# Down projection of two ConvGLU layers: 16 of 22 inner tiles by a seven-product scheme

## The chip, the cores and the metric

The kernel runs on one core of one Trainium2 chip. The metric is the device time of one execution in microseconds, the median of several runs. Engines are named TensorE (PE in the rows; PEld is its weight load), VectorE (DVE), ScalarE (ACT), GpSimd (POOL) and SyncE (SP), whose queue issues nearly all DMAs.

## The reference

One step of a two-layer encoder over 1024 prompt and 32 sample tokens, model width 1024, float32: a gated linear attention layer, then a latent attention layer, each followed by a ConvGLU of inner width 2816. The change touches the two ConvGLUs alone:

```python
def conv_glu(h, prev, w_in, conv_w, conv_b, w_out):
    g, u = jnp.split(h @ w_in, [D_FF], axis=-1)
    gc, new_prev = causal_dwconv(g, prev, conv_w, conv_b)
    return (jax.nn.gelu(gc, approximate=False) * u) @ w_out, new_prev
...
    x = x + o
    h = rmsnorm(x, norm_ffn[l])
    o, prev = conv_glu(h, ffn_prev0[l], w_ffn_in[l], ffn_conv_w[l], ffn_conv_b[l], w_ffn_out[l])
    x = x + o
```

## The kernel before, in words

Activations lie transposed in SBUF: rows of 128 features (KD = 8 for the model, NF = 22 for the inner width), T = 1056 token columns. Every product of two float32 operands is made of three float32r matmuls: each operand is split into a rounded part (hi, by a ScalarE copy) and a remainder (lo, by a subtraction on VectorE or GpSimd), and hi x hi, hi x lo and lo x hi are added in PSUM (`mm3`, L339, and `product`, L752).

A ConvGLU runs as a list of units. Unit f makes gate and up rows of inner tile f. Unit 0 is plain. Units 1 to 21 use a seven-product scheme (Winograd's form of Strassen's): the operand x is a 2 x 2 block matrix of 4 rows by 528 columns, the weights likewise with gate and up as the two output rows. Four sums of weight quarters (`s_sums`, L978, VectorE) and four sums of x blocks, T1 to T4 (once per layer), feed seven products P1 to P7 of 24 matmuls of 128x264, in the order of `ORDER`: P1, P2, P6, P5, P7, P4, P3. ScalarE copies three results out of PSUM (`snap`), VectorE adds the others (`gate_left`, `up_right`, `up_left`, `gate_right`), then come the convolution (`conv`, L1070, VectorE, five operations), the GELU (ScalarE) and the product with up (`glu`, VectorE). SP stores the finished activation of each tile in DRAM (`sp_a_out`, L659, to s_a). x itself has been stored in DRAM (s_x), since the scratch of the units covers its rows in SBUF.

The down projection (`pe_ffn`, L867) then goes over 11 groups of two inner tiles. For each group SP loads 1 MB of weights and the two activations (`sp_a_in`), ScalarE and GpSimd split both, and TensorE makes 24 output tiles of 128x352 (8 rows, three column chunks), 6 matmuls each, 144 a group. VectorE adds each tile to x; in the first group it adds to x read back from DRAM into two places of 4 rows (xback), which SP loads during unit 21.

Two weight slots alternate over units and groups. The order of each engine is written out by hand; engines wait for each other by counting semaphores. SP's queue too is in program order: a wait in it (`prod(f, n)`: product number n of unit f is done) holds all DMAs behind it.

## Time and profile before

| | |
|---|---|
| median of 3 runs | 2638.41 us (2638.26 to 2638.42) |
| the profiled execution | 2640.56 us, its span 2638.7 us |
| TensorE's mean granted clock in it | 0.995 of full speed |
| matmuls | 18206 |
| DMA | 221.93 MB, mean 84 GB/s |

The span is the time from the first to the last instruction. The profile gives each engine's busy time, the chain of waits that ended last, groups of instructions by source line, and the issue of DMAs with their time to landing. Durations of matmuls overlap each other, so what a matmul costs is read from how many fit in a stretch of time.

### The profile page before, as it was taken

How to read it: one execution, taken by the hardware profiler on the slowest of the kernel's cores; microseconds unless marked ns; L12 is line 12 of the kernel's file. 1: busy time of each engine (PE TensorE's matmuls, PEld its weight loads, DVE VectorE, ACT ScalarE, POOL GpSimd, SP SyncE). 2: the span in 40 equal slices, each digit the busy share in tenths (PEclk: the TensorE clock that was granted, in tenths of full speed). 3: DMA queues.
4: the chain of work that ended last, by engine and by line, in shares of the span. 5: the costliest groups of instructions: out<-in, count | busy, mean ns of one | idle time of the engine just before them, and what ended most of it. 6: DMA issues, size and time to landing. Idle time of an engine off the chain costs nothing.

```text
span 2638.7 us, 43372 instructions
## 1 busy us (share of the span) xinstructions
PE 2579.3 (98%) x18206; PEld 2500.3 (95%) x18206; DVE 1487.2 (56%) x2660; ACT 1000.7 (38%) x1651; POOL 932.6 (35%) x546
## 2 busy tenths in 40 slices
PE   8999999999999999999999989999999999999999
PEld 7999999999999999999998988889999999999999
DVE  6735353578555455555625875555696555446554
ACT  6333333364233322111547756444453233321111
POOL 5121212152433444444522223223334433444441
PEclk9999999999999999999999999999999999999999
DMA  3111111122222224222213253132122222233222
GB/s 110 35 37 35 37 39 34 38 98 81 81 74 90 74 81 180 74 98 98 70 45 126 108 198 124 49 98 73 61 71 82 81 73 89 74 136 117 98 98 100
DMA packets 182159, 221.93 MB, mean 84 GB/s; under 512 B 16690, under 2 KB 145344, under 8 KB 181328
## 3 DMA queue, kind: packets, MB, share of 16 engines
q1 hardware_dynamic: 179567, 217.08, 24.5%
q8 instruction: 144, 2.36, 0.4%
q10 hardware_dynamic: 2400, 2.10, 0.3%
q14 instruction: 48, 0.39, 0.0%
HBM read 160.56 MB, written 58.59 MB: 83 GB/s over the span
## 4 chain that ended last, share of the span: by engine, by line
PE 89%; DVE 6%; ACT 2%; issue 1%; DMA 1%; SPq 0%; POOL 0%; DVEq 0%; ACTq 0%; POOLq 0%
PE ps L341 14%; PE ps L343 13%; PE ps L342 13%; PE ps L758 11%; PE ps L760 11%; PE ps L759 11%; PE ps L2366 3%; PE ps L1289 1%; PE ps L2350 1%; PE ps L1276 1%; PE ps L1277 1%; PE ps L1278 1%; DVE xT L585 1%; PE ps L1365 1%; PE ps L1348 1%
## 5 line engine op out<-in xcount | busy, mean ns | idle before, releaser
L585 DVE TENSOR_TENSOR xT<-xT,ps 128x352 f32<-128x352 f32 x672 | 347.2, 519 | 249.2 <-PE ps L343 248.1
L1170 POOL TENSOR_TENSOR wlo<-wraw,whi 128x1024 fp32r<-128x1024 f32 x78 | 187.3, 2401 | 454.7 <-DVE s_raw L993 454.7
L306 POOL TENSOR_TENSOR wlo<-wraw,whi 128x2048 fp32r<-128x2048 f32 (+1 forms) x37 | 168.3, 4550 | 498.2 <-ACT whi L299 468.8
L341 PE MATMUL ps<-fahi,whi 128*128 128x352 f32 x960 | 311.1, 324 | 0.1
L343 PE MATMUL ps<-fahi,wlo 128*128 128x352 f32 x960 | 308.1, 321 | 0.0
L342 PE MATMUL ps<-falo,whi 128*128 128x352 f32 x960 | 307.9, 321 | 0.0
L299 ACT ACTIVATE whi<-wraw 128x2048 fp32r<-128x2048 f32 x40 | 76.6, 1914 | 396.7 <-DMA wraw<-w_ffn_out 328.1
L341 PE MATMUL ps<-hh,whi 128*128 128x352 f32 x648 | 218.5, 337 | 0.6 <-ACT cqr L2679 0.3
L343 PE MATMUL ps<-hh,wlo 128*128 128x352 f32 x648 | 208.2, 321 | 0.0
L342 PE MATMUL ps<-hl,whi 128*128 128x352 f32 x648 | 207.9, 321 | 0.0
L758 PE MATMUL ps<-hh,whi 128*128 128x264 f32 x672 | 191.5, 285 | 0.4 <-DVE wlo L1019 0.4
L759 PE MATMUL ps<-hl,whi 128*128 128x264 f32 x672 | 191.2, 285 | 0.0
L760 PE MATMUL ps<-hh,wlo 128*128 128x264 f32 x672 | 191.2, 284 | 0.0
L341 PEld LDWEIGHTS ps<-fahi,whi 128*128 128x128 f32 x960 | 180.1, 188 | 0.9 <-DVE xT L585 0.4
L342 PEld LDWEIGHTS ps<-falo,whi 128*128 128x128 f32 x960 | 180.4, 188 | 0.2
L343 PEld LDWEIGHTS ps<-fahi,wlo 128*128 128x128 f32 x960 | 180.3, 188 | 0.0
L1170 POOL TENSOR_TENSOR s_lo<-s_raw,s_hi 128x512 fp32r<-128x512 f32 x80 | 148.4, 1855 | 60.0 <-ACT s_hi L890 60.0
L1047 DVE TENSOR_TENSOR hf<-hf,ps 128x528 f32<-128x528 f32 x42 | 29.6, 704 | 188.6 <-ACT hf L926 188.6
L758 PEld LDWEIGHTS ps<-hh,whi 128*128 128x128 f32 x672 | 126.5, 188 | 1.3 <-DVE wlo L1019 0.8
L341 PEld LDWEIGHTS ps<-hh,whi 128*128 128x128 f32 x648 | 121.6, 188 | 5.7 <-issue 2.6
L760 PEld LDWEIGHTS ps<-hh,wlo 128*128 128x128 f32 x672 | 126.6, 188 | 0.0
L759 PEld LDWEIGHTS ps<-hl,whi 128*128 128x128 f32 x672 | 126.4, 188 | 0.0
(414 smaller groups left out, 7920.0 us busy)
## 6 DMA issues: line engine op xcount, KB each, us to landing
wraw<-w_ffn_in SPq DMA_DIRECT2D x88, 512.0 KB, 3.8
s_a<-hf SPq DMA_DIRECT2D x44, 528.0 KB, 3.3
wraw<-w_ffn_out SPq DMA_DIRECT2D x44, 512.0 KB, 4.3
fa<-s_a SPq DMA_DIRECT2D x40, 528.0 KB, 6.1
wraw<-w_gla_in SPq DMA_DIRECT2D x24, 512.0 KB, 4.6
s_x<-xT SPq DMA_DIRECT2D x6, 1408.0 KB, 5.8
xback<-s_x SPq DMA_DIRECT2D x4, 2112.0 KB, 12.1
s_k<-kw SPq DMA_DIRECT2D x8, 784.0 KB, 3.3
```

Source lines behind the costliest of these rows:

```text
L299: act.activation(hi[:, 0:cols], raw[:, 0:cols], ACT.Copy).then_inc(S("w_hi"), 1)
L306: pool.tensor_tensor(lo[:, 0:cols], raw[:, 0:cols], hi[:, 0:cols].bitcast(F32), ALU.subtract).then_inc(S("w_lo"), 1)
L341: nc.tensor.matmul(out, w[0], x[0], start=start, stop=False)
L342: nc.tensor.matmul(out, w[0], x[1], start=False, stop=False)
L343: return nc.tensor.matmul(out, w[1], x[0], start=False, stop=stop)
L585: dve.tensor_tensor(xT[:, m, tc(j)], xT[:, m, tc(j)], ps[:, banks[i % len(banks)], 0:TC], ALU.add)\
L758: nc.tensor.matmul(out, w_[0], x_[0], start=first, stop=False, skip_group_check=True)
L759: nc.tensor.matmul(out, w_[0], x_[1], start=False, stop=False, skip_group_check=True)
L760: last = nc.tensor.matmul(out, w_[1], x_[0], start=False, stop=(k == HK - 1), skip_group_check=True)
L1047: dve.tensor_tensor(right, left, two(U_SIDE), ALU.add).then_inc(S("summed"), 1)
L1170: return pool.tensor_tensor(lo[:, cols], raw[:, cols], hi[:, cols].bitcast(F32), ALU.subtract)
L2366: last = pe.matmul(ps[:, 6, 0:m], av[h % 2][0:n, kk0 // P, :], aPT[s % 2][0:n, i, 0:m], start=(i == 0), stop=(i == len(tiles) - 1))
```

## The change

Inner tiles 1 to 16 of the down projection now go through the same seven-product scheme, in two chunks of eight inner tiles (ND = 8 units a layer, units 22 to 29; four per chunk, each unit making one pair of output rows, `PAIRS`). The x operand of a chunk is again a 2 x 2 block matrix: X11 and X21 are odd and even inner tiles, left half of the columns, X22 the even tiles' right half, T1 to T4 their sums. The sums are made by VectorE in the gate/up phase (`pair_sum`, four operations of 528 columns for each two units) and stored in DRAM (s_t). At the turn from unit 21 to 22, and from 25 to 26, SP loads seven blocks of 4 rows by 528 columns (`sp_block`) into the places of the old operands, each after the product that last reads the place; ScalarE rounds them (`refill`), VectorE subtracts for five of them and GpSimd for T3 and X22 (`block_lo`). No result is copied out of PSUM: VectorE adds the products straight into x (`into_x`, seven adds of 528 columns a unit). x is read back into its own rows in four pairs (`sp_x_in`). The other six inner tiles (0 and 17 to 21) stay plain, as three groups of two. In the down units VectorE makes all weight sums and remainders; their places are parts of the activation rows (S4), of x operand rows (S2, S3) and of the convolution's row (S3 of odd units).

Each unit's weight sums wait as the diff shows: for units 22 and 23 (`f in (NF, NF + 1)`) the fourth sum waits until all stores of even, or odd, tiles have landed, since it writes into those activation rows.

```diff
+        PAIRS = ((3, 4), (0, 1), (2, 5), (6, 7))
+        BLOCKS = (("X11", "X21", "T2", "T1", "T3", "T4", "X22"), ("X11", "X21", "T2", "T1", "T3", "X22", "T4"))
...
+        def sp_block(sp, layer, part, i):
+
+            name, n = BLOCKS[part][i], 7 * part + i
+            if A_LOADS * layer + n >= 2:
+                before, count = load_count(layer, n - 2)
+                sp.wait_ge(S(before), nth(before, count))
+            if name[0] == "T":
+                sp.wait_ge(S("t_stored"), nth("t_stored", 16 * (NT * layer + 4 * part + 4)))
+                src = A["s_t"][4 * part:4 * part + 4, :, ("T1", "T3", "T2", "T4").index(name), :].rearrange("q p t -> p q t")
+            else:
+                odd = name == "X11"
+                sp.wait_ge(S(f"a_stored{int(odd)}"), nth(f"a_stored{int(odd)}", 16 * (NFG * layer + 4 * part + 4 + (not odd))))
+                first, t0 = ND * part + (1 if odd else 2), TH if name == "X22" else 0
+                src = A["s_a"][first:first + ND - 1:2, :, t0:t0 + TH].rearrange("q p t -> p q t")
+            sem, _ = load_count(layer, n)
+            sp.dma_start(xblock(name)[1], src).then_inc(S(sem), 16)
...
-            sp_a_in(sp, layer, 0)
+            sp_block(sp, layer, 0, 0)
+            prod(f, 2)
+            sp_block(sp, layer, 0, 1)
+            sp_next_w(sp, layer, c0, f + 2, 0)
+            sp_x_in(sp, layer, 0)
             prod(f, 3)
-            sp.dma_start(xback[0][:, :, :], A["s_x"][:, 0:HK, :]).then_inc(S("x_back0"), 16)
+            sp_block(sp, layer, 0, 2)
             sp_a_out(sp, layer, f - 1)
-            prod(f, 4)
-            sp_a_in(sp, layer, 1)
-            prod(f, 5)
-            sp.dma_start(xback[1][:, :, :], A["s_x"][:, HK:KD, :]).then_inc(S("x_back1"), 16)
-            prod(f, 6)
-            sp_w_out(sp, layer, c0, 1)
+            for n in (4, 5, 6):
+                prod(f, n)
+                sp_block(sp, layer, 0, n - 1)
+            sp_next_w(sp, layer, c0, f + 2, 1)
+            prod(f, 7)
+            sp_block(sp, layer, 0, 6)
+            sp_x_in(sp, layer, 1)
+            sp.wait_ge(S("conv"), NF * layer + NF - 1)
+            sp_x_in(sp, layer, 2)
+            for f in range(NF, NF + ND):
+                last = f == NF + ND - 1
+                for n in range(1, 8):
+                    if n in (2, 7) or f == NF + 3 or last and n in (3, 4):
+                        prod(f, n)
+                    if f == NF + 3:
+                        sp_block(sp, layer, 1, n - 1)
+                    if last and n in (3, 4):
+                        sp_a_in(sp, layer, n - 3)
+                    if n in (2, 7):
+                        sp_next_w(sp, layer, c0, f + 2, n // 7)
+                if f == NF:
+                    sp.wait_ge(S("conv"), NF * (layer + 1))
+                    sp_x_in(sp, layer, 3)
+                    sp_a_out(sp, layer, NF - 1)
             sp_a_in(sp, layer, 2)
-            sp_a_out(sp, layer, f)
-            for g in range(2, NFG):
-                sp.wait_ge(S("down_mm"), 24 * (b0 + g - 1))
-                sp_w_out(sp, layer, c0, g)
-                if g > 2:
-                    sp_a_in(sp, layer, g)
+            sp.wait_ge(S("down_mm"), 24 * (b0 + 1))
+            for kk in range(2):
+                sp_w_out(sp, layer, c0, 2, kk)
...
-            for g in range(1, NFG - 1):
-                pe_down_ffn(pe, layer, chunk(c0 + NF + g), 24 * (b0 + g), g)
-            pe_down_ffn(pe, layer, chunk(c0 + NF + NFG - 1), 24 * (b0 + NFG - 1), NFG - 1,
+            for f in range(NF, NF + ND):
+                pe_unit_down(pe, layer, chunk(c0 + f), f)
+            pe.wait_ge(S("summed"), cnt("summed", layer, NF + ND - 1, 6))
+            pe_down_ffn(pe, layer, chunk(c0 + NF + ND), 24 * b0, 0, banks=FIRST_BANKS)
+            pe_down_ffn(pe, layer, chunk(c0 + NF + ND + 1), 24 * (b0 + 1), 1)
+            pe_down_ffn(pe, layer, chunk(c0 + NF + ND + 2), 24 * (b0 + 2), 2,
...
+            def refill(part, f, early, late):
+
+                block_hi(part, 0)
+                early()
+                block_hi(part, 1)
+                side_hi(f, "S2")
+                late()
+                block_hi(part, 2)
+                block_hi(part, 3)
+                w_hi_side(f)
+                block_hi(part, 4)
+                side_hi(f, "S3")
+                side_hi(f, "S4")
+                block_hi(part, 5)
+                block_hi(part, 6)
...
+                if 2 < f < NF:
+                    dve.wait_ge(S("prod"), cnt("prod", layer, f - 1, 0))
+                if f == NF:
+                    dve.wait_ge(S("t_stored"), nth("t_stored", 16 * NT * (layer + 1)))
+                if f > NF:
+                    dve.wait_ge(S("prod"), cnt("prod", layer, f - 1, 3))
+                if f == NF + 1:
+                    dve.wait_ge(S("glu"), NF * (layer + 1))
                 dve.tensor_tensor(s3, w[0], w[2], ALU.subtract).then_inc(S("s_sum"), 1)
-                dve.wait_ge(S("s_sum"), nth("s_sum", 4 * u + 1))
+                dve.wait_ge(S("s_sum"), cnt("s_sum", layer, f, 1))
                 dve.tensor_tensor(w[2], w[2], w[3], ALU.add).then_inc(S("s_sum"), 1)
-                dve.wait_ge(S("s_sum"), nth("s_sum", 4 * u + 2))
+                dve.wait_ge(S("s_sum"), cnt("s_sum", layer, f, 2))
                 dve.tensor_tensor(s2, w[2], w[0], ALU.subtract).then_inc(S("s_sum"), 1)
-                dve.wait_ge(S("s_sum"), nth("s_sum", 4 * u + 3))
+                dve.wait_ge(S("s_sum"), cnt("s_sum", layer, f, 3))
+                if f in (NF, NF + 1):
+                    stored = f"a_stored{f % 2}"
+                    dve.wait_ge(S(stored), nth(stored, 16 * NFG * (layer + 1)))
                 dve.tensor_tensor(s4, w[1], s2, ALU.subtract).then_inc(S("s_sum"), 1)
...
+                s_sums(f + 1)
+                if f == NF - 1:
+                    w_low_in(f + 1)
+                    block_lo(0, 0)
+                    block_lo(0, 1)
+                pair = (f - 3) // 2 if f % 2 and f <= 2 * NT + 1 else None
+                if pair is not None:
+                    pair_sum(pair, "T1")
+                    pair_sum(pair, "T3")
+                up_right(f)
+                if f == NF - 1:
+                    block_lo(0, 2)
+                up_left(f)
+                if pair is not None:
+                    pair_sum(pair, "T2")
+                    pair_sum(pair, "T4")
+                gate_right(f)
+                if f < NF - 1:
+                    conv(f)
+
+            for f in range(NF, NF + ND):
+                part, first, more = (f - NF) // 4, (f - NF) % 4 == 0, f + 1 < NF + ND
+                side_lo(f, "S2")
+                if first:
+                    into_x(f, 1)
+                    block_lo(part, 3)
+                w_low_side(f)
+                if not first:
+                    into_x(f, 1)
+                side_lo(f, "S3")
+                if f == NF:
+                    conv(NF - 1)
+                into_x(f, 2)
+                if f > NF:
+                    side_lo(f, "S4")
+                into_x(f, 3)
+                if f == NF:
+                    side_lo(f, "S4")
+                if first:
+                    into_x(f, 4)
+                    block_lo(part, BLOCKS[part].index("T4"))
+                    if f == NF:
+                        glu(NF - 1)
+                    into_x(f, 5)
                     s_sums(f + 1)
-                up_right(f)
-                up_left(f)
-                gate_right(f)
-                conv(f)
-
+                    into_x(f, 6)
+                    w_low_in(f + 1)
+                    into_x(f, 7)
+                    continue
+                if more:
+                    s_sums(f + 1)
+                into_x(f, 4)
+                if f == NF + 3:
+                    block_lo(1, 0)
+                    into_x(f, 5)
+                    w_low_in(f + 1)
+                    block_lo(1, 1)
+                    into_x(f, 6)
+                    block_lo(1, 2)
+                else:
+                    if more:
+                        w_low_in(f + 1)
+                    into_x(f, 5)
+                    into_x(f, 6)
+                into_x(f, 7)
...
+            for part in range(2):
+                for name in ("T3", "X22"):
+                    block_lo(part, name)
+            pool_split(pool, chunk(c0 + NF + ND), WC)
+            a_low(0)
+            a_low(1)
+            pool_split(pool, chunk(c0 + NF + ND + 1), WC)
+            a_low(2)
+            pool_split(pool, chunk(c0 + NF + ND + 2), WC)
```

The order of instructions at the places where the operands turn over. First SP's queue of layer 0 before, from the last DMAs of unit 20 on through unit 21; wraw is a weight slot, hf the activation rows, h and fa the places where activations are loaded.

```order
L661 DMA s_a<-hf_219 256x1x528
L328 DMA wraw_56<-w_ffn_out 128x1024 x2
L668 DMA h_52<-s_a 128x2x528 x2
L717 DMA xback_130<-s_x 128x4224
L661 DMA s_a<-hf_219 256x1x528
L671 DMA fa_137<-s_a 128x1056 x2
L722 DMA xback_131<-s_x 128x4224
```

The same place now, from the second product of unit 21 through the end of unit 22; h and hflat are the places of the seven blocks, and just ahead of the first row stand the loads of X11 and X21 (L740, h from s_a, twice).

```order
L332 DMA wraw_55<-w_ffn_out 128x8x128
L758 DMA xT<-s_x 128x2112
L740 DMA hflat<-s_t 128x4x528
L719 DMA s_a<-hf_220 256x1x528
L740 DMA hflat<-s_t 128x4x528 x3
L332 DMA wraw_55<-w_ffn_out 128x8x128
L740 DMA h_52<-s_a 128x4x528
L758 DMA xT<-s_x 128x2112
L758 DMA xT<-s_x 128x2x1056
L332 DMA wraw_56<-w_ffn_out 128x8x128 x2
L758 DMA xT<-s_x 128x2112
L719 DMA s_a<-hf_220 256x1x528
```

The store of tile 20 (the first L719) stood behind the load of xback and now stands behind block X21, a weight half, a pair of x rows and block T2, and the store of tile 21 (the last row) behind the weights issued after the last product of unit 22 and the last x pair.

VectorE's queue now, in unit 21 of layer 0 (before, the right half of up, L1047, followed `glu` at once in this unit):

```order
L1261 TENSOR_TENSOR fg_111<-fg_111,ps 128x528
L1320 TENSOR_TENSOR hf_220<-hf_220,fc 128x2x528
L1189 TENSOR_TENSOR h_52<-wraw_56 128x512
L1191 TENSOR_TENSOR wraw_56<-wraw_56 128x4x128
L1193 TENSOR_TENSOR h_52<-wraw_56 128x512
L1198 TENSOR_TENSOR hf_220<-wraw_56,h_52 128x512
L1239 TENSOR_TENSOR wlo_58<-wraw_56,whi_54 128x1024
L1326 TENSOR_TENSOR hl<-h_52,hh 128x4x528 x2
L1266 TENSOR_TENSOR hf_220<-hf_220,ps 128x528
L1326 TENSOR_TENSOR T2lo<-hflat,T2hi 128x2112
L1272 TENSOR_TENSOR hf_220<-hf_220,ps 128x528
```

L1189 to L1198 are the four weight sums of unit 22, L1239 its low half, L1326 the remainders of blocks, L1266 the right half of up of unit 21: the sums, the low half and two remainders now stand ahead of it.

## Rows read from the trace of the kernel before

**Rows 1.** The page, parts 1 and 4: busy time, and the chain by engine.
```profile
PE 2579.3 (98%) x18206; PEld 2500.3 (95%) x18206; DVE 1487.2 (56%) x2660; ACT 1000.7 (38%) x1651; POOL 932.6 (35%) x546
PE 89%; DVE 6%; ACT 2%; issue 1%; DMA 1%; SPq 0%; POOL 0%; DVEq 0%; ACTq 0%; POOLq 0%
```

**Rows 2.** Timeline of TensorE, layer 0: start, duration, line, tiles, form.
```profile
988.58 0.28 PE L758 MATMUL ps<-hh,whi 128*128 128x264 f32 x1
...
1009.00 0.28 PE L758 MATMUL ps<-hh,whi 128*128 128x264 f32 x1
...
1029.41 0.32 PE L341 MATMUL ps<-hhf,whi 128*128 128x352 f32 x1
```

**Rows 3.** Windows of TensorE: length, busy (count), granted clock, DMA share, GB/s.
```profile
670.00:990.00 320.00, 320.00 (x2636) 1.00 0.25 80
1060.00:1260.00 200.00, 200.00 (x1258) 1.00 0.24 86
```

**Rows 4.** Timeline of VectorE in units 20 and 21 of layer 0.
```profile
998.66 0.69 DVE L993 TENSOR_TENSOR s_raw<-wraw,s_raw 128x512 f32<-128x512 f32 x1
1004.03 0.70 DVE L1047 TENSOR_TENSOR hf<-hf,ps 128x528 f32<-128x528 f32 x1 [4.67 <-ACT hf L926]
...
1010.03 0.82 DVE L1080 TENSOR_SCALAR fc<-fg,par 128x1056 f32<-128x1056 f32 x1
1010.89 1.28 DVE L1083 SCALAR_TENSOR_TENSOR fc<-fg,par,fc 128x1024 f32<-128x1024 f32 x1
...
1013.58 0.25 DVE L1093 SCALAR_TENSOR_TENSOR fc<-sm,par,fc 128x32 f32<-128x32 f32 x1
```

**Rows 5.** Splitting: by source line, count, duration in ns min/median/max, first and last start.
```profile
L939 ACT ACTIVATE fahi<-fa x20: 1948/1972/1976, 1040.9 to 2589.7; 128x2112 fp32r<-128x2112 f32 x20
L1015 DVE TENSOR_TENSOR T1lo<-hflat,T1hi x2: 2345/2347/2349, 603.2 to 1948.0; 128x2112 fp32r<-128x2112 f32 x2
L1019 DVE TENSOR_TENSOR wlo<-wraw,whi x6: 1212/1218/1226, 592.5 to 1958.4; 128x1024 fp32r<-128x1024 f32 x6
L1195 POOL TENSOR_TENSOR falo<-fa,fahi x20: 4742/4758/4781, 1045.7 to 2592.4; 128x2112 fp32r<-128x2112 f32 x20
```

**Rows 6.** DMA issues: whole span (KB, median us to landing), SP's timeline, that store.
```profile
wraw<-w_ffn_in SPq DMA_DIRECT2D x88, 512.0 KB, 3.8
s_a<-hf SPq DMA_DIRECT2D x44, 528.0 KB, 3.3
...
1017.97 0.34 SPq L717 DMA_DIRECT2D xback<-s_x  x1
1018.35 0.56 SPq L661 DMA_DIRECT2D s_a<-hf  x1
...
s_a<-hf SPq DMA_DIRECT2D x1, 528.0 KB, 9.3
```

**Rows 7.** Window with DMA full; PE, PEld, DVE, ACT, POOL, clock, DMA share, GB/s.
```profile
1019.00:1041.00 22.00, 22.00 (x161) 22.00 (x160) 11.98 (x23) 5.02 (x5) 7.18 (x2) 1.00 0.99 387
```

**Rows 8.** VectorE beside GpSimd: timeline after unit 1; two lines over the whole span.
```profile
616.43 2.40 POOL L1170 TENSOR_TENSOR wlo<-wraw,whi 128x1024 fp32r<-128x1024 f32 x1
617.54 1.86 DVE L1080 TENSOR_SCALAR fc<-fg,par 128x1056 f32<-128x1056 f32 x1
618.79 2.83 POOL L1170 TENSOR_TENSOR s_lo<-s_raw,s_hi 128x1024 fp32r<-128x1024 f32 x1
619.43 3.27 DVE L1083 SCALAR_TENSOR_TENSOR fc<-fg,par,fc 128x1024 f32<-128x1024 f32 x1
...
L987 DVE TENSOR_TENSOR s_raw<-wraw x42: 676/684/1418, 584.3 to 2341.3; 128x512 f32<-128x512 f32 x42
L1047 DVE TENSOR_TENSOR hf<-hf,ps x42: 697/704/706, 616.1 to 2369.3; 128x528 f32<-128x528 f32 x42
```

**Rows 9.** TensorE's restart in unit 2 of layer 0: timeline row, then windows.
```profile
625.33 0.56 PE L758 MATMUL ps<-T2hi,s_hi 128*128 128x264 f32 x1 [4.32 <-ACT fg L926]
...
625.00:628.00 3.00, 2.67 (x12) 0.50 0.02 5
```

More of the change, by code:

```diff
@@ L53 @@
 NFG = NF // 2
+ND = 8
+NT = ND
+NG2 = 3
+NLO = 2 * 2 + NG2
 NU = NF - 1
@@ L663, in sp_a_in @@
         def sp_a_in(sp, layer, g):
+            before, count = load_count(layer, 14 + g - 2)
+            sp.wait_ge(S(before), nth(before, count))
             for i in range(2):
[L665 to L671 removed]
+                sp.wait_ge(S(f"a_stored{i}"), nth(f"a_stored{i}", 16 * NFG * (layer + 1)))
@@ L862, in pe_down_ffn @@
         def pe_down_ffn(pe, layer, c, before, g, after=None, banks=C_BANKS):
-            pe.wait_ge(S("a_lo"), NFG * layer + g + 1)
-            down_pe(pe, c, before, [fahi[g % 2][:, k, :] for k in range(2)],
-                    [falo[g % 2][:, k, :] for k in range(2)], after=after, banks=banks)
+            pe.wait_ge(S("a_lo"), NLO * layer + 4 + g + 1)
+            down_pe(pe, c, before, [fahi[g][:, k, :] for k in range(2)],
+                    [falo[g][:, k, :] for k in range(2)], after=after, banks=banks)
@@ L924, in snap @@
                     act.wait_ge(S(f"a_stored{f % 2}"), nth(f"a_stored{f % 2}", 16 * (NFG * layer + f // 2)))
+                    if 3 <= f <= 2 * NT + 2:
+                        q, last = (f - 3) // 2, 2 if f % 2 else 4
+                        act.wait_ge(S("t_sum"), nth("t_sum", T_SUMS * layer + 4 + 4 * q + last))
                 dst = a_rows(f)[:, 0, :] if n == 2 else fg[f % 2][:, 2 + n * TH:2 + (n + 1) * TH]
@@ L1101, in glu, with block_lo, side_lo, into_x @@
                 dve.tensor_tensor(v, v, fc[:, :].rearrange("p (b t) -> p b t", b=2), ALU.mult).then_inc(S("glu"), 1)
+            def block_lo(part, i):
+                hi, raw, lo = xblock(BLOCKS[part][i])
+                dve.wait_ge(S("t_hi"), nth("t_hi", T_HIS * layer + 4 + 7 * part + i + 1))
+                dve.tensor_tensor(lo, raw, hi.bitcast(F32), ALU.subtract).then_inc(S("t_lo_dve"), 1)
+            def side_lo(f, name):
+                dve.wait_ge(S("s_hi"), cnt("s_hi", layer, f, {"S2": 1, "S3": 3, "S4": 4}[name]))
+                hi, raw, lo = side(name, f)
+                dve.tensor_tensor(lo, raw, hi.bitcast(F32), ALU.subtract).then_inc(S("s_lo"), 1)
+            def into_x(f, n):
+                p = (f - NF) % 4
+                m, half, bank, same = {1: (0, 0, sum_bank(f), 0), 2: (0, 0, U_DOWN, 1), 3: (0, 1, sum_bank(f), 0),
+                                       4: (1, 1, U_SIDE, 0), 5: (1, 1, sum_bank(f), 4), 6: (0, 1, U_SIDE, 3),
+                                       7: (1, 0, sum_bank(f), 0)}[n]
+                if n == 1 and f < NF + 4:
+                    sem = f"x_back{p % 2}"
+                    dve.wait_ge(S(sem), nth(sem, 16 * (2 * layer + p // 2 + 1)))
+                if same:
+                    dve.wait_ge(S("summed"), cnt("summed", layer, f, same))
+                dve.wait_ge(S("prod"), cnt("prod", layer, f, n))
+                row = two_of(xT[:, PAIRS[p][m], half * TH:(half + 1) * TH])
+                dve.tensor_tensor(row, row, two(bank), ALU.add).then_inc(S("summed"), 1)
             dve.wait_ge(S("x_spilled"), nth("x_spilled", 16 * NCH * (layer + 1)))
```

394 lines of the change are left out of this document (244 added, 150 removed).

## The prediction

> **What bounds the kernel now.** I read the page's first part and its chain of waits first: TensorE is busy for 98% of the span and makes 89% of the chain that ended last [rows 1]. So one microsecond of TensorE work is one microsecond of time as long as nobody makes TensorE wait, and the whole question is how many matmuls the change takes away and how many waits it puts in. Next I read TensorE's timeline at the turn from gate/up to down projection in layer 0 [rows 2]. Two gate/up units start at 988.58 and 1009.00 and the down projection at 1029.41, so a seven-product unit (168 matmuls of 264 columns) lasts 20.42 us, one product of 24 matmuls 2.92 us, without a gap. The windows by stage [rows 3] give the price of one matmul: 320 us for 2636 of 264 columns, 121.4 ns each, and 200 us for 1258 of 352 columns, 159.0 ns each; their mean durations on the page are longer because they overlap, and are not the price. A group of 144 is thus 22.9 us. I call the products of a unit by position: 1 ends 2.92 us into it, 3 at 8.75, 7 at 20.42.
>
> **What goes.** Per layer 16 of 22 inner tiles leave the plain scheme: 8 groups of 22.92 us, 183.4 us. In come 8 units of 20.42 us, 163.3 us. TensorE's own work shrinks by 20.1 us a layer, 40.2 us in all. If nothing waited, that would be the gain.
>
> **What is hidden.** In gate/up VectorE gets four sums of 528 columns for two units, some 0.7 us each, and SP a store of 1.08 MB (four rows of 528 columns, 128 partitions, 4 bytes). VectorE is free from the end of its weight sums (999.3) to the right half of up (1004.0) [rows 4], so this stays covered; only in unit 3, where VectorE is late, I count 0.3 us. Inside the steady down units VectorE does about 12 us (seven operations of 512 columns at 0.69, two of 1024 at 1.22, seven adds at 0.70) of 20.4, ScalarE 4: covered. The x rows come back in time for their first add.
>
> **What is new on the path.** All of it lies where operands turn over: seven blocks of 1.08 MB, each loaded once the last product of its old content is done, rounded by ScalarE (1.95 us) and subtracted from by VectorE (2.35 us) or GpSimd (4.76 us) [rows 5]. The prices of a transfer: the store of a tile (0.54 MB) lands 3.3 us after issue when alone, but 9.3 us after issue when it stood 0.38 us behind the 2.16 MB of xback [rows 6]. That is 1.7 us fixed plus 338 GB/s; the same stretch moved 387 GB/s at a 0.99 share [rows 7]. Transfers of the one queue hence land in turn, and I take 360 GB/s. A weight half (0.52 MB in rows of 512 bytes) lands in 3.8 us, so 0.5 us more each.
>
> *Stall A, last product of unit 21.* The fourth weight sum of unit 22 goes into the place of tile 20's activation and waits for that store to land. SP issues the store only after product 3, behind block X21, a weight half, an x pair and block T2: from the issue of X21 at 1015.0, 4.31 MB, 1.7 + 12.0 + 0.5 = 14.2 us, landing at 1029.2. Behind this wait on VectorE stand the sum (0.69), the low half (1.22), two blocks (2 x 2.35) and then the right half of up (0.70), for which TensorE waits before product 7: 1036.6 instead of 1009.00 + 17.50 = 1026.5. Stall 10.1 us (9.2 at 387 GB/s, 10.8 at 338).
>
> *Stall C, first product of unit 23.* The same with tile 21, and worse, as SP issues that store only after the last product of unit 22, behind a weight half and the last x pair: 0.2 + 1.7 + 2.15 MB (6.0) + 0.5 = 8.4 us; then the sum, one add into x and the low half (0.69 + 0.70 + 1.22, gaps 0.2). TensorE has nothing in between: stall 11.2 us.
>
> *Stall B, product 5 of unit 22.* It needs VectorE's add of product 3. VectorE adds product 1 at 3.0, then come block T1, a weight half, a difference, the convolution of tile 21 (1010.03 to 1013.83, with the copy ahead 3.9 us [rows 4]), the adds of products 2 and 3: 3.0 + 0.70 + 2.35 + 1.22 + 0.69 + 3.9 + 1.4 = 13.3 against the 11.7 us at which TensorE is ready. But GpSimd subtracts blocks T3 and X22 just then, and VectorE's operations that read SBUF alone wait until GpSimd's running instruction ends: TENSOR_SCALAR took 1.86 us for 0.82, SCALAR_TENSOR_TENSOR 3.27 for 1.28, a 512-column sum 1.42 for 0.68, while adds from PSUM stay at 0.70 [rows 4, 8]. T3 runs until about 2.9 and costs 0.6, X22 falls into the convolution and costs its 4.76: 18.7. Stall 7.0 us. Bounds: 1.6 without these waits, 11.1 with two whole ones.
>
> *Stall D, unit 26,* where the second chunk's blocks come in: no store is waited for, but the same two GpSimd subtractions. T3, the fifth block, lands 1.7 + 5.93 MB (16.5) + 0.5 us after the first issue (2.9 us into unit 25) and is rounded 3.2 to 3.6 us into unit 26; VectorE has its first add done at 4.2 and waits until 8.4. Block T1 and the weight half end at 11.9, wanted at 8.75 (3.1 us). Then a difference and an add, X22 until 17.4, a difference and the add of product 3: 18.8, wanted at 14.9 (3.9 us). Sum 7.0, bounds 0 and 8.
>
> *The clock.* After the 4.32 us pause in unit 2 the granted clock was 0.50, 1.2 GHz, from 625 to 628; twelve matmuls ran where 22 would have at 121.4 ns [rows 9]: 1.2 us lost. A, B, C and D each bring one such restart: 4.8 us. With 0.3 us in unit 3 and 0.4 us before the first plain group:
>
> per layer 10.1 + 7.0 + 11.2 + 7.0 + 0.7 + 4.8 - 20.1 = **+20.7 us**, both layers +41.4 us. The profiled span was 2638.7 us (the execution 2640.6), the median of the runs 2638.4; I add to the median: **2680 us**.
>
> The Trainium skill, page DMA: Bandwidth & Descriptors, section Specifications, gives a fabric ceiling of 435 GB/s and an HBM limit of about 358 GB/s per core. By the ceiling, estimated, A would be 2.1 us and C 1.0 us shorter per layer and the sum 2674; the row of 338 GB/s sides with the lower figure, single windows of 387 lie between.
>
> **Rivals.**
> 1. *GpSimd does not hold VectorE.* Then B is 1.6 us and too short for a restart at 1.2 GHz, D is gone: 10.1 + 1.6 + 11.2 + 0.7 + 2.4 - 20.1 = +5.9 a layer, 2650 us. For it: no row shows a VectorE block subtraction beside GpSimd's, and VectorE may get in between. Against it: [rows 8]. Chance 0.25. The Trainium skill, GPSIMD Engine Reference, section Specifications, says that GpSimd's SBUF interfaces are shared with VectorE for instructions with two SBUF inputs; the trace agrees (1.86 us for 0.82 [rows 8]), which lowers this rival's chance.
> 2. *The stores are not in turn (other side).* If a tile's store lands in its lone 3.3 us despite the queue ahead of it, A's sum is free at 1021.7 and the right half of up done at 1029.1 (stall 2.6 us), and C is 1.3 + 3.3 + 2.8 = 7.4 us. With rival 1's B and D and one restart: 2.6 + 1.6 + 7.4 + 0.7 + 1.2 - 20.1 = -6.6 a layer, 2625 us. It decides where A and C together fall under some 16 us. Against it: the 9.3 us landing [rows 6]. If the two waits on stores were never last, the sum would go to 2600. Chance 0.06.
> 3. *More turn-over waits than I found*, as block X22, last of the seven, subtracted on GpSimd and wanted 14.6 us into unit 22: 2690 to 2710 us. Chance 0.10.
> 4. Little difference because a slower queue and a gain cancel: 0.03. The forecast itself has 0.56.
>
> **How the numbers follow.** Range: rival 1 at 387 GB/s gives 2647, so 2646; upward the forecast at 338 GB/s (+1.1 a layer) with B at its bound (+4.1) gives 2690. It leaves out 0.15. A measurement tells about 0.2% (5 us) from no change. Faster 0.06, same 0.03, slower 0.91.
>
> **What would show it.** Per layer, pauses of TensorE before the last product of unit 21 (waiting for VectorE's right half of up, itself behind a weight sum that waits for the DMA of a tile), before product 5 of unit 22, before product 1 of unit 23 (10 to 12 us) and in unit 26; PEclk under 9 in those slices. The first product of each steady down unit must follow the last of the unit before at once, 20.4 us apart, else the saving itself is wrong. VectorE subtractions of 2112 elements longer than 2.35 us would show the GpSimd wait. No pause over 5 us at units 21 and 23 would refute the forecast.

## The result and the profile after

| | before | changed |
|---|---|---|
| median | 2638.41 us (2638.26 to 2639.78, 4 runs) | 2689.38 us (2687.67 to 2689.58, 4 runs) |
| ratio, 95% interval | 1 | 1.019 [1.0175, 1.0205] |
| span of the profiled execution | 2638.7 us | 2687.6 us |
| mean granted clock | 0.995 | 0.981 |

The change costs 51 us; 41 were forecast. The page, parts 1 and 4, against [rows 1]:

```profile
PE 2560.2 (95%) x18590; PEld 2477.3 (92%) x18590; DVE 1655.2 (62%) x2616; ACT 1051.6 (39%) x1727; POOL 840.4 (31%) x522
PE 83%; DVE 10%; DMA 3%; issue 2%; ACT 2%; SPq 0%; POOL 0%; DVEq 0%; ACTq 0%; POOLq 0%
```

TensorE falls from 98% to 95% of a longer span, and VectorE and DMA have 13% of the chain instead of 7%. TensorE's timeline of layer 0, where it paused for 2 us or more between unit 21 and unit 26, and the starts of units 24 and 25 (unit 24 begins at 1106.30):

```profile
1038.49 0.59 PE L863 MATMUL ps<-hh,s_hi 128*128 128x264 f32 x1 [10.61 <-DVE hf L1266]
...
1061.71 0.56 PE L863 MATMUL ps<-T3hi,hl 128*128 128x264 f32 x1 [5.78 <-DVE xT L1346]
...
1083.50 0.59 PE L863 MATMUL ps<-hh,whi 128*128 128x264 f32 x1 [11.41 <-DVE wlo L1239]
...
1106.30 0.28 PE L863 MATMUL ps<-hh,whi 128*128 128x264 f32 x1
...
1126.72 0.28 PE L863 MATMUL ps<-hh,whi 128*128 128x264 f32 x1
...
1159.03 0.36 PE L863 MATMUL ps<-T1hi,whi 128*128 128x264 f32 x1 [2.97 <-DVE wlo L1239]
...
1165.97 0.36 PE L863 MATMUL ps<-T3hi,hl 128*128 128x264 f32 x1 [2.35 <-DVE xT L1346]
```

These are stalls A, B, C and the two of D, at the products that the forecast named. Units 24 and 25 are 20.42 us apart: a down unit that waits for nothing costs what a gate/up unit does [rows 2]. In layer 1 the five pauses are 10.47, 5.76, 11.89, 2.97 and 3.80 us. Behind each, the clock. Windows of TensorE from the start of four products on (length, busy and count, granted clock, DMA share, GB/s), then one steady unit, then two products of layer 1, behind A and behind the first pause of D, and last the product in unit 2 behind the pause that the kernel before has too:

```profile
1038.49:1043.90 5.41, 5.41 (x24) 0.50 0.33 95
1061.71:1066.10 4.39, 4.39 (x25) 0.66 0.01 4
1083.50:1088.80 5.30, 5.30 (x24) 0.52 0.00 0
1159.03:1165.90 6.87, 4.58 (x24) 0.75 0.00 0
...
1106.30:1126.70 20.40, 20.40 (x170) 1.00 0.18 53
...
2406.70:2411.00 4.30, 4.30 (x24) 0.66 0.42 120
2527.48:2530.40 2.92, 2.92 (x24) 1.00 0.02 6
...
625.14:630.56 5.42, 5.42 (x25) 0.50 0.13 51
```

24 matmuls, 2.92 us at full clock [rows 3], take 5.3 to 5.4 us behind A and C of layer 0, where the granted clock was 0.50 to 0.52 (1.2 GHz). In layer 1 the product behind A takes 4.3 us (0.66) although the pause is as long, and the one behind D's first pause, 2.97 us in both layers, takes 2.92 us at 1.00, where it lost 1.4 us in layer 0. The forecast had 1.2 us for each restart, from [rows 9].

**Stall A on VectorE:** the weight sums of unit 22, two blocks' remainders, then the right half of up; and the one store behind it (L719, all 44 stores of tiles):

```profile
1019.54 0.69 DVE L1193 TENSOR_TENSOR h<-wraw 128x512 f32<-128x512 f32 x1
1031.26 0.69 DVE L1198 TENSOR_TENSOR hf<-wraw,h 128x512 f32<-128x512 f32 x1 [11.03 <-DMA s_a<-hf]
1032.06 1.23 DVE L1239 TENSOR_TENSOR wlo<-wraw,whi 128x1024 fp32r<-128x1024 f32 x1
1033.20 4.62 DVE L1326 TENSOR_TENSOR hl<-h,hh 128x2112 fp32r<-128x2112 f32 x2
1037.74 0.70 DVE L1266 TENSOR_TENSOR hf<-hf,ps 128x528 f32<-128x528 f32 x1
```

```profile
L719 SPq DMA_DIRECT2D s_a<-hf x44: 524/525/996, 628.7 to 2440.9; - x44
...
  DVE hf L1198: 46.1, 4
...
DMA to landing us min/median/max: 3.1/3.4/11.5
```

The DMA engines were full all the while (TensorE's window from X21's issue to the landing, columns as above):

```profile
1016.30:1031.10 14.80, 11.58 (x96) 0.98 1.04 378
```

The store that lands 3.4 us after issue elsewhere took 11.5 here. VectorE waited four times for stores, 46.1 us in all: A and C of both layers.

**Stall B**, VectorE and GpSimd in unit 22, and **stall D**, VectorE in unit 26:

```profile
1050.17 1.22 DVE L1239 TENSOR_TENSOR wlo<-wraw,whi 128x1024 fp32r<-128x1024 f32 x1
1051.30 0.68 DVE L1331 TENSOR_TENSOR hl<-h,hl 128x512 fp32r<-128x512 f32 x1
1051.91 4.71 DVE L1295 COPY sm<-fg 128x32 f32<-128x32 f32 x1
1056.54 0.82 DVE L1299 TENSOR_SCALAR fc<-fg,par 128x1056 f32<-128x1056 f32 x1
...
1051.53 5.05 POOL L1488 TENSOR_TENSOR hl<-h,hh 128x2112 fp32r<-128x2112 f32 x1 [6.24 <-ACT hh L1103]
...
1153.14 5.75 DVE L1239 TENSOR_TENSOR wlo<-wraw,whi 128x1024 fp32r<-128x1024 f32 x1
1158.81 5.18 DVE L1331 TENSOR_TENSOR hl<-h,hl 128x512 fp32r<-128x512 f32 x1
```

A copy of 32 columns, 0.18 us in nearly every other unit, lasts 4.71 us and ends at 1056.62, as GpSimd's subtraction does at 1056.58. In unit 26 a remainder of 1.22 us takes 5.75 and one of 0.68 takes 5.18, 4.5 us more each: GpSimd's two instructions beside them. It goes the other way too: T3 on GpSimd, started 0.3 us after VectorE's subtraction of T2 (1038.35, 2.35 us), takes 6.62 us instead of 4.76:

```profile
1038.67 6.62 POOL L1488 TENSOR_TENSOR T3lo<-hflat,T3hi 128x2112 fp32r<-128x2112 f32 x1 [29.62 <-ACT T3hi L1103]
```

The Trainium skill, page SBUF — State Buffer, section SBUF: two separate sides, says that of a VectorE operation with two SBUF inputs, or in a two-port mode, and a GpSimd operation the one that starts first gets the pair of ports for the whole instruction while the other blocks. By that rule B and D are waits for whole GpSimd instructions, and the trace agrees in both directions (4.71 us for 0.18 on VectorE, 6.62 for 4.76 on GpSimd).

**Stall C:**

```profile
1068.42 0.69 DVE L1193 TENSOR_TENSOR h<-wraw 128x512 f32<-128x512 f32 x1
1081.00 0.69 DVE L1198 TENSOR_TENSOR hf<-wraw,h 128x512 f32<-128x512 f32 x1 [11.89 <-DMA s_a<-hf]
1081.61 0.70 DVE L1346 TENSOR_TENSOR xT<-xT,ps 128x528 f32<-128x528 f32 x1
1082.22 1.22 DVE L1239 TENSOR_TENSOR wlo<-wraw,whi 128x1024 fp32r<-128x1024 f32 x1
```

The last product of unit 22 ends at 1083.50 - 11.41 = 1072.1, and tile 21's store has landed 8.9 us later; forecast 8.4.

### The profile page after: what moved, and what is told of

Its sections match the earlier page's. It is cut to its first block, busy times and chain, and to the rows that moved or that the text cites. A ratio compares the mean times of both kernels' runs of the same rounds, so it can differ in the third digit from the quotient of the medians.

```text
span 2687.6 us, 44342 instructions
## 1 busy us (share of the span) xinstructions
PE 2560.2 (95%) x18590; PEld 2477.3 (92%) x18590; DVE 1655.2 (62%) x2616; ACT 1051.6 (39%) x1727; POOL 840.4 (31%) x522
## 4 chain that ended last, share of the span: by engine, by line
PE 83%; DVE 10%; DMA 3%; issue 2%; ACT 2%; SPq 0%; POOL 0%; DVEq 0%; ACTq 0%; POOLq 0%
PE ps L863 14%; PE ps L865 14%; PE ps L864 14%; PE ps L345 9%; PE ps L347 8%; PE ps L346 8%; PE ps L2668 3%; DMA s_a<-hf 1%; PE ps L1591 1%; PE ps L2652 1%; PE ps L1578 1%; PE ps L1579 1%; PE ps L1580 1%; DVE xT L589 1%; PE ps L1667 1%
## 5 line engine op out<-in xcount | busy, mean ns | idle before, releaser
L863 PE MATMUL ps<-hh,whi 128*128 128x264 f32 x928 | 267.2, 288 | 24.1 <-DVE wlo L1239 24.1
L864 PE MATMUL ps<-hl,whi 128*128 128x264 f32 x928 | 266.1, 287 | 0.0
L589 DVE TENSOR_TENSOR xT<-xT,ps 128x352 f32<-128x352 f32 x336 | 172.1, 518 | 103.4 <-PE ps L347 102.2
L1346 DVE TENSOR_TENSOR xT<-xT,ps 128x528 f32<-128x528 f32 x112 | 78.2, 701 | 109.4 <-PE ps L865 108.9
L863 PE MATMUL ps<-T1hi,whi 128*128 128x264 f32 x464 | 133.0, 287 | 6.0 <-DVE wlo L1239 5.9
L864 PE MATMUL ps<-T1lo,whi 128*128 128x264 f32 x464 | 132.6, 286 | 0.0
L865 PE MATMUL ps<-T1hi,wlo 128*128 128x264 f32 x464 | 132.4, 285 | 0.0
L863 PE MATMUL ps<-T4hi,whi 128*128 128x264 f32 x464 | 132.0, 284 | 0.0
L864 PE MATMUL ps<-T4lo,whi 128*128 128x264 f32 x464 | 131.8, 284 | 0.0
L865 PE MATMUL ps<-T4hi,wlo 128*128 128x264 f32 x464 | 131.5, 283 | 0.0
```

The source lines that it names most:

```text
L589: dve.tensor_tensor(xT[:, m, tc(j)], xT[:, m, tc(j)], ps[:, banks[i % len(banks)], 0:TC], ALU.add)\
L863: nc.tensor.matmul(out, w_[0], x_[0], start=first, stop=False, skip_group_check=True)
L864: nc.tensor.matmul(out, w_[0], x_[1], start=False, stop=False, skip_group_check=True)
L865: last = nc.tensor.matmul(out, w_[1], x_[0], start=False, stop=(k == HK - 1), skip_group_check=True)
L1346: dve.tensor_tensor(row, row, two(bank), ALU.add).then_inc(S("summed"), 1)
```

## The experiments

Two questions: is each pause the mechanism that the forecast gave it, and what is left when all are gone? The kernel before ran beside each set (medians 2640.86, 2639.78 and 2640.74 us), so ratios are compared. The sum of the pauses gone need not be the time gained, since a pause lets blocks arrive.

| run | median us | ratio to before, 95% |
|---|---|---|
| s4_22: no store wait in unit 22's sums | 2681.07 | 1.0154 [1.0135, 1.0172] |
| s4_23: none in unit 23's | 2661.40 | 1.0082 [1.0061, 1.0102] |
| s4_both: none in either | 2647.63 | 1.0027 [1.0015, 1.0039] |
| store_early: tile 20's store earlier in SP's queue | 2680.04 | 1.0148 [1.0128, 1.0169] |
| pool_pieces: GpSimd's T3 and X22 in four pieces each | 2690.43 | 1.0200 [1.0183, 1.0217] |
| alldve: T3 and X22 on VectorE | 2662.72 | 1.0087 [1.0071, 1.0102] |
| reordered: s4_both, VectorE's queue in another order | 2649.84 | 1.0040 [1.0026, 1.0054] |
| reordered_alldve: the same, T3 and X22 on VectorE | 2626.59 | 0.9947 [0.9933, 0.9961] |
| s4_both_alldve: s4_both, T3 and X22 on VectorE | 2636.84 | 0.9985 [0.9976, 0.9994] |
| best_again: reordered_alldve again | 2624.97 | 0.9942 [0.9928, 0.9955] |

### The store waits (A and C)

The fourth weight sum gets a place in x's columns whose pair is read back later, so that nothing waits for a store:

```diff
+            if n == "S4" and f in (NF, NF + 1,):
+                at_ = 6144 + f % 2 * (T + 8 + 24)
+                return x4r[:, at_ + QB:at_ + 2 * QB], x4[:, at_:at_ + QB], x4r[:, at_:at_ + QB]
...
-                if f in (NF, NF + 1):
+                if f in (NF + 2, NF + 3):
...
-            sp.wait_ge(S("conv"), NF * layer + NF - 1)
-            sp_x_in(sp, layer, 2)
...
+                    sp_x_in(sp, layer, 2)
                     sp.wait_ge(S("conv"), NF * (layer + 1))
-                    sp_x_in(sp, layer, 3)
                     sp_a_out(sp, layer, NF - 1)
+                if f == NF + 1:
+                    sp_x_in(sp, layer, 3)
```

That is the version with both; the first run has it for unit 22 alone, the second for unit 23 alone.

> The fourth weight sum of unit 22 is put into x's idle rows 5 and 6, so it waits for no store; x pair 2 is loaded after unit 22. Theory (the pause before the last product of unit 21 is the wait for tile 20's store): that pause of 10.5 us goes to under 1 us and with it its restart at 1.2 GHz (1.4 to 2.5 us). Unit 22 then starts some 12 us sooner, and the pause before unit 23 grows by up to 3 us, since one more x pair stands ahead of tile 21's store; the pause in unit 22 gets a little longer. 2672 to 2678 us. Rival (VectorE and the queue are simply full at this turn, and any wait removed comes back at the next product): 2685 us or more, the pause before product 7 of unit 21 being replaced by one of about the same size before products 1 to 3 of unit 22.

Measured 2681.07. Pause A is gone (0 and 1.06 us in the two layers), but B grew to 11.22 and 10.70 and C to 13.86 and 13.66. It lies between theory and rival. In the changed kernel pause A had held unit 22 back until GpSimd's T3 (1038.67 to 1045.29) was nearly done. Without A unit 22 starts 13 us sooner, T3 starts when it did (1038.88), and so it falls beside unit 22's VectorE work, as in the version with both, shown below. C grew as forecast, since one more x pair (1.08 MB) now stands ahead of tile 21's store.

> The fourth weight sum of unit 23 is put into x's idle rows 6 and 7, so it waits for no store; x pair 3 is loaded after unit 23. Theory (the pause before unit 23 is the wait for tile 21's store): that pause of 11.4 to 11.9 us goes to under 1 us with its restart of 2.4 us, nothing else changes: 12 to 13.5 us a layer, 2662 to 2666 us. Rival (VectorE is late anyway, having a whole unit's work behind it): a pause of 5 us or more stays before unit 23, 2675 us or more.

Measured 2661.40, as the theory says. C is gone entirely, unit 23 follows unit 22 at once; A (9.93, 10.55) and B (5.78) stay. This and the run before are the two that show a store wait by itself.

> Both places moved. Theory: pauses before the last product of unit 21 and before unit 23 under 2 us each; left are the pause in unit 22 (about 7 us) and those in unit 26 (5.3 to 6.8 us). 2645 to 2652 us, still above the kernel before. Rival (full VectorE): the two gains do not add, 2660 us or more.

Measured 2647.63. A and C are gone, 7 us remain over the kernel before, which took 2640.86 beside it. VectorE and GpSimd of this version in unit 22 of layer 0, and TensorE's one pause there:

```profile
1037.67 5.22 DVE L1336 TENSOR_TENSOR hl<-h,hl 128x512 fp32r<-128x512 f32 x1
...
1044.95 4.62 DVE L1309 SCALAR_TENSOR_TENSOR fc<-sm,par,fc 128x32 f32<-128x32 f32 x1
...
1037.10 5.23 POOL L1493 TENSOR_TENSOR T3lo<-hflat,T3hi 128x2112 fp32r<-128x2112 f32 x1 [29.92 <-ACT T3hi L1108]
1044.06 5.46 POOL L1493 TENSOR_TENSOR hl<-h,hh 128x2112 fp32r<-128x2112 f32 x1 [1.73 <-ACT hh L1108]
...
1052.44 0.56 PE L868 MATMUL ps<-T3hi,hl 128*128 128x264 f32 x1 [11.38 <-DVE xT L1351]
```

Two operations of 0.68 and 0.25 us now wait out two GpSimd instructions, 4.5 and 4.4 us. One more such wait on top of the changed kernel's 5.8 us gives 10.3; the rest probably comes from block T2, whose remainder falls into unit 22 now (1028.97) and not ahead of it. So B of 11.4 us is the forecast's upper bound for it ("11.1 with two whole ones"), reached once A no longer puts unit 22 behind T3. The time lies where it was expected, but not for the reason given: B was expected to be 7 us. In layer 1 the unit paused for 3.61 us ahead of its fourth product and 5.47 ahead of its fifth.

The same from SP's side, the store of tile 20 right behind block X21 instead of behind 2.7 MB more:

```diff
             sp_block(sp, layer, 0, 1)
+            sp_a_out(sp, layer, f - 1)
             sp_next_w(sp, layer, c0, f + 2, 0)
             sp_x_in(sp, layer, 0)
             prod(f, 3)
             sp_block(sp, layer, 0, 2)
-            sp_a_out(sp, layer, f - 1)
```

> Only SP's order changes: the store of tile 20 is issued ahead of the weight half, the x pair and block T2 (2.7 MB less ahead of it). Theory (transfers of the queue land in turn at about 360 GB/s): the store lands some 7 us sooner, the pause before the last product of unit 21 falls from 10.5 to 2 to 3.5 us, all else stays: 2674 to 2677 us. Rival (the store's landing does not depend on what stands ahead of it, or something else holds VectorE): the pause stays over 8 us, 2686 us or more.

Measured 2680.04, less gained than expected. A fell from 10.61 to 2.48 us: the store's place in the queue makes A. But unit 22 has a new pause of 3.03 us, ahead of its fourth product, beside B's 5.55 (3.40 and 5.49 in layer 1); "all else stays" was wrong. TensorE at that pause, and VectorE's remainder of the weight half that this product reads:

```profile
1044.30 0.36 PE L863 MATMUL ps<-T1hi,whi 128*128 128x264 f32 x1 [3.03 <-issue]
```

```profile
1038.48 5.72 DVE L1239 TENSOR_TENSOR wlo<-wraw,whi 128x1024 fp32r<-128x1024 f32 x1
...
1045.67 5.59 DVE L1302 SCALAR_TENSOR_TENSOR fc<-fg,par,fc 128x1024 f32<-128x1024 f32 x1
```

TensorE's row names no releaser, but the remainder ends at 1044.20, 0.1 us before it, and is 4.5 us too long: again T3 on GpSimd (1037.02 to 1043.12), which in the changed kernel ran mostly ahead of unit 22.

### GpSimd and VectorE (B and D)

```diff
-                pool.tensor_tensor(lo, raw, hi.bitcast(F32), ALU.subtract).then_inc(S("a_lo"), 1)
+                for i in range(HK):
+                    last = pool.tensor_tensor(lo[:, i, :], raw[:, i, :], hi[:, i, :].bitcast(F32), ALU.subtract)
+                last.then_inc(S("a_lo"), 1)
```

> The changed kernel, with each of the four remainders of blocks T3 and X22 that GpSimd takes cut into four instructions of a quarter (132x4 columns) each; nothing else differs. Theory (the pause of 5.78 us ahead of the fifth product of unit 22 is VectorE waiting until a whole GpSimd instruction of 4.76 us is over): VectorE gets in between the pieces, so the pause ahead of product 5 falls to 2 to 3.5 us, and the GpSimd work itself ends later, with waits of GpSimd's remainders in its place ahead of later products of units 22 and 26 (up to 7 us in unit 26). Time 2680 to 2690 us. Rival (VectorE is simply overloaded there, GpSimd does not hold it): the pause of unit 22 stays at 5.5 to 6 us and unit 26 at 5 to 7 us, and the time stays within 2 us of the changed kernel's 2689.

Measured 2690.43: no gain, and the theory's pause of 2 to 3.5 us did not come. B stayed (5.42 us) as the rival says, but not for its reason. VectorE in unit 22 and GpSimd beside it:

```profile
1049.90 1.30 DVE L1295 COPY sm<-fg 128x32 f32<-128x32 f32 x1
1051.11 1.89 DVE L1299 TENSOR_SCALAR fc<-fg,par 128x1056 f32<-128x1056 f32 x1
1053.04 2.22 DVE L1302 SCALAR_TENSOR_TENSOR fc<-fg,par,fc 128x1024 f32<-128x1024 f32 x1
1055.19 1.28 DVE L1304 SCALAR_TENSOR_TENSOR fc<-sm,par,fc 128x32 f32<-128x32 f32 x1
...
1049.43 6.99 POOL L1489 TENSOR_TENSOR hl<-h,hh 128x528 fp32r<-128x528 f32 x4 [5.48 <-ACT hh L1103]
```

Alone these four take 0.18, 0.82, 1.28 and 0.25 us. They do get in between the pieces, but one at a time, each waiting out a piece: 1.12 + 1.07 + 0.94 + 1.03 = 4.2 us lost, against 4.5 in one wait. Cut into four, the instruction shares its hold out and does not reduce it; GpSimd takes 7.0 us instead of 5.05, and unit 26 gets a 4.86 us wait for it. The next run takes GpSimd out altogether:

```diff
-T_HIS, T_LOS, T_SUMS = 4 + 14 + NG2, 4 + 2 * 5, 4 + 4 * NT
+T_HIS, T_LOS, T_SUMS = 4 + 14 + NG2, 4 + 2 * 7, 4 + 4 * NT
...
-                if f == NF:
-                    conv(NF - 1)
                 into_x(f, 2)
+                if first:
+                    block_lo(part, BLOCKS[part].index("T3"))
...
+                    block_lo(part, BLOCKS[part].index("X22"))
                     into_x(f, 4)
                     block_lo(part, BLOCKS[part].index("T4"))
+                    into_x(f, 5)
                     if f == NF:
+                        conv(NF - 1)
                         glu(NF - 1)
-                    into_x(f, 5)
```

(GpSimd's `block_lo` and TensorE's waits on it go; TensorE waits on VectorE's count.)

> The changed kernel, with the four remainders of T3 and X22 moved from GpSimd to VectorE (2.35 us each there), the glu and convolution of tile 21 behind them; stores and weight sums as in the changed kernel. Theory (GpSimd's instructions hold VectorE): the pauses of 5.8 us in unit 22 and of 5.3 to 6.8 us in unit 26 shrink to under 2.5 us each although VectorE has 4.7 us more to do per group of blocks; the pause at the end of unit 21 (10.6) and the one ahead of unit 23 (11.4) stay. About 10 to 12 us less per layer, 2663 to 2672 us. Rival (VectorE is overloaded, no hold): the pauses of units 22 and 26 grow by about the 4.7 us added each, 2700 to 2712 us.

Measured 2662.72, 13 us a layer less than the changed kernel (10 to 12 were expected) with 9.4 us a layer more work on VectorE. In place of B there is this pause, and the longest 512-column remainder of the kind that took 5.18 us is now the third number of the second row (ns, min/median/max):

```profile
1058.08 0.36 PE L863 MATMUL ps<-hh 128*128 128x264 f32 x1 [0.28 <-DVE xT L1342]
...
L1327 DVE TENSOR_TENSOR hl<-h,hl x24: 682/684/686, 1043.7 to 2558.7; 128x512 fp32r<-128x512 f32 x24
```

Unit 26 fell from 29.2 to 22.3 us; A (9.95, 10.32) and C (10.66, 11.11) stayed. For D that settles it: VectorE got 4.7 us more to do in unit 26, half of it ahead of the fifth product, and both pauses went (1.20 us ahead of unit 27 came), where a merely overloaded VectorE wanted the reverse. For B the run is weaker evidence, because the convolution of tile 21 (4 us), which stood ahead of the adds that B waits for, went behind them too. That B is GpSimd's hold rests on the copy's 4.71 us for 0.18 and on the two holds of the version above.

### Can the seven products pay?

The last versions rest on the one with both store waits gone. Two things vary: who makes the remainders of T3 and X22, and the order of VectorE's queue in units 21 to 26, written out as a list. Each of the two reordered versions has a list of its own (here the first lines in the version without GpSimd; `s_sum(f, n)` is the n-th sum of `s_sums(f)`):

```python
glu(NF - 2); gate_left(NF - 1); s_sum(NF, 1); block_lo(0, "X11"); s_sum(NF, 2); s_sum(NF, 3)
block_lo(0, "X21"); up_right(NF - 1); s_sum(NF, 4); up_left(NF - 1); side_lo(NF, "S2")
w_low_in(NF); gate_right(NF - 1); block_lo(0, "T2"); into_x(NF, 1); conv(NF - 1); into_x(NF, 2)
w_low_side(NF); block_lo(0, "T1"); into_x(NF, 3); side_lo(NF, "S3"); block_lo(0, "T3")
```

> The version with the fourth weight sums of units 22 and 23 in x's own columns (both store waits gone), and VectorE's queue of units 21 to 26 in another order: weight sums of unit 22 and 23 ahead of the blocks' remainders, the convolution of tile 21 early, and additions into x as their products come. Theory (what is left over the kernel before is VectorE's order in two crowded units, 11.4 us in unit 22 and 6.8 us in unit 26 of the version without the store waits): pauses of unit 22 and the start of unit 23 sum to 7 to 10 us, unit 26 to 2 to 4 us, time 2622 to 2634 us, under the kernel before by 0.2 to 0.6%. Rival (VectorE's load, not its order, sets it): the pauses only change places and the time stays at 2640 to 2650 us.

Measured 2649.84: the theory missed by 16 us, and the time is the rival's. Its pauses in unit 22 and ahead of unit 23 sum to 8.9 us as expected (2.87, 3.06, 0.67, 1.41, 0.92 in layer 0), but unit 26 still pauses for 1.50 and 3.78 us, and slow products behind the pauses took back the rest. TensorE in unit 22 of this version, of s4_both, and of the fastest version:

```profile
1031.81:1065.18 33.37, 24.44 (x171) 0.90 0.48 170
```

```profile
1028.72:1062.89 34.17, 22.51 (x171) 0.85 0.50 174
```

```profile
1031.96:1058.76 26.80, 21.63 (x171) 1.00 0.64 223
```

Pauses fell from 11.4 to 8.9 us, yet the unit only from 34.2 to 33.4 us: over it the granted clock was 0.90, and one pause had become five. GpSimd still held VectorE here (a remainder of 0.68 us took 5.20 at 1048.29).

> As the reordered version, but all seven remainders of both groups of blocks on VectorE and none on GpSimd, with an order of its own. Theory (GpSimd holds VectorE for as long as its instruction runs, 4.76 us for what VectorE does in 2.35): 2 to 3 us per layer better than the reordered version, pauses of unit 22 and the start of unit 23 sum to 6 to 8 us, unit 26 to 1 to 3 us, time 2618 to 2630 us. Rival (GpSimd's share is free help): 4 x 2.35 us more VectorE work per layer makes it slower than the reordered version by 5 us or more.

Measured 2626.59, and 2624.97 when repeated: faster than both kernels, 0.5 to 0.6% under before.

> Both store waits gone and all block remainders on VectorE, but VectorE's queue in the changed kernel's own order (with the convolution and glu of tile 21 behind the remainders, as in the version that has only the remainders moved): with the runs already made it completes a table of two by two, GpSimd's share kept or not, queue reordered or not. Theory (the two gains need each other: without GpSimd's instructions the crowded stretch is VectorE's own 26.7 us in a unit of 20.4, and reordering only helps where VectorE isn't held): unit 22's pauses and the one ahead of unit 23 sum to 7 to 10 us, nearly all ahead of unit 23, unit 26 costs 22.3 us; time 2634 to 2642 us, level with the kernel before. Rival (the order did the work in the fastest version): no better than 2645 us.

Measured 2636.84, 0.9985 [0.9976, 0.9994], level with the kernel before within 0.2%. Unit 26 is 22.28 us long; the pauses of unit 22 and ahead of unit 23 sum to 10.9 and 10.5 us, a little over the expected 7 to 10, 7.71 of them ahead of unit 23.

> The fastest version once more, for its ratio to the kernel before in a second set of runs: 0.993 to 0.997, if the first set's 0.9947 was no accident; over 0.998 if it was.

With GpSimd's share the other order gained nothing (1.0027, 1.0040); without it the other order is worth 0.4% (0.9985, 0.9947). GpSimd's share costs 0.4% in the old order and 0.9% in the new. The comparison is not a clean one of two factors, since taking GpSimd out moved the convolution in the first pair and changed the whole list in the second; another list with GpSimd's share might do better. Windows of unit 22 in layer 0 (TensorE, its weight load, VectorE, ScalarE, GpSimd) in s4_both_alldve and in the fastest version:

```profile
1030.45:1062.66 32.21, 21.28 (x171) 20.53 (x169) 28.46 (x32) 14.45 (x14) 0.00 (x0) 0.93 0.71 252
```

```profile
1031.96:1058.76 26.80, 21.63 (x171) 20.61 (x169) 26.37 (x29) 14.00 (x14) 0.00 (x0) 1.00 0.64 223
```

In the fastest version VectorE is busy for 26.4 of 26.8 us: unit 22 of layer 0 is now bound by its work, and 6.4 us over a steady unit is what is left of stalls A, B and C there.

## Why the prediction was right, and where its sizes were off

Per layer, the forecast's terms against the trace of the changed kernel:

| term | forecast us | layer 0 | layer 1 |
|---|---|---|---|
| TensorE's own work | -20.1 | -20.1 | -20.1 |
| A | 10.1 | 10.61 | 10.47 |
| B | 7.0 | 5.78 | 5.76 |
| C | 11.2 | 11.41 | 11.89 |
| D | 7.0 | 2.97 + 2.35 | 2.97 + 3.80 |
| clock at 1.2 GHz | 4.8 | 10.5 | 8.9 |
| units before 21 (forecast 0.3) and the first plain group (0.4) | 0.7 | 1.2 | 1.6 |
| sum | 20.7 | 24.7 | 25.3 |

The clock term is the rest of units 21, 22, 23 and 26: they last 33.76 + 39.56 + 22.80 + 29.19 = 125.3 us, less 4 x 20.42 and less 33.1 us of pauses, 10.5; small waits are in it. Start to start of their matmuls, the five products behind the pauses lost 9.5 and 8.1 us; the other 1.0 and 0.8 us of this row are small waits and the ends of the last matmuls before them. In layer 0, 1.1 of the 1.2 us before unit 21 are the clock again: unit 2's product behind its old pause took 5.4 us where it took 4.3 in the kernel before.

The two sums are 50 us; the span grew by 48.9. From the first gate/up product to the last plain group the two ConvGLUs grew by 25.3 and 25.6 us, and the stage between them took 1.9 us less.

- **Saving: right.** 20.42 us for a unit, from starts and ends of steady ones.
- **Stall A: right,** 0.5 us short. The store landed 11.5 us after issue. From X21's issue (1016.23, with TensorE 1.2 us later than before) to landing 14.9 us pass, for 14.2; less 1.7 and 0.5, 4.31 MB in 12.7 us would be 339 GB/s, as in the store's own row. But the sum left out what still stood ahead: X11, issued at 1013.31, landed 5.9 us later, at 1019.2, and some 0.6 MB of it (an estimate from the bytes moved until 1016.23) came first. With them the rate is 387, and the window of those 14.8 us shows 378 GB/s. So the 0.5 us can be the rate or the bytes, and no run separates them. The Trainium skill, page DMA: Bandwidth & Descriptors, section Specifications, has an HBM limit of about 358 GB/s and a ceiling of 435. The forecast let a rate of 338 side with the lower figure; the window of 378 lies above it, as [rows 7] does, so the trace does not agree with that limit for this kernel.
- **Stall B: right in its mechanism,** 1.2 us too large. GpSimd's X22 fell into the copy ahead of the convolution and cost 4.5 us. T3, forecast at 0.6 us, cost nothing on the path: it held a difference for 0.4 us in layer 0 (1.6 in layer 1) while VectorE's next add had to wait for TensorE's first product anyway. That so little was left of T3 was owed to pause A, which had put unit 22 behind it. The forecast had this cover in its sum and named two whole waits only as a bound; the run without A showed them.
- **Stall C: right,** 11.4 and 11.9.
- **Stall D: right in its place and both waits;** the first was 2.97 us for 3.1, the second 2.35 us in layer 0 and 3.80 in layer 1, for 3.9.
- **The clock: the mis-sized term,** "A, B, C and D each bring one such restart: 4.8 us". It was short by 5.7 and 4.1 us, the whole sum by 4.0 and 4.6. The 3 us window that it was read from did little harm, since the whole product behind the same pause took 4.27 us in the kernel before, 1.4 us lost for 1.2. Two other things failed. D has two pauses, so there are five restarts. And one price was taken for all, where the price varies: start to start, in layers 0 and 1, A cost 2.7 and 1.4 us, B 1.5 and 2.3, C 2.4 and 2.7, D 1.4 and 0.1 for its first pause and 1.6 for its second. It varies between pauses as long as each other (10.61 and 10.47 us) and even for the old pause in unit 2, so the length of the pause alone does not set it. What does, no run here shows.
- **Luck in the sum.** B and D were put 2.9 us too high in layer 0 and 1.5 in layer 1, which hid part of the clock's error. The measured 2689.4 lies just under the forecast's upper end of 2690, but that end was made of B at its bound and a slow queue, and it was the clock that took the time there.
- **A sign that did not come.** "VectorE subtractions of 2112 elements longer than 2.35 us": all 20 took 2.34 to 2.35 us. GpSimd's instructions held a copy and three subtractions of 512 and 1024 columns in each layer instead; the hold was real, but its place was misread.
- **Rivals.** Rival 1 is refuted by 4.71 us for 0.18 and, for D, by the run without GpSimd's share; of its rows, that of 1.86 us is an operation with one SBUF input, and the one with two is the 3.27 us for 1.28 beside it. Rival 2 is refuted by the landing of 11.5 us and by the 2.48 us that A fell to when the store alone moved up the queue. Of rival 3, nothing was found, though its time (2690) was nearly met: X22 on GpSimd was not waited for in the changed kernel.
